# Recurrent mixer's end: outputs of two chunks at a time, q's squares added on VectorE, two gate tiles behind the sums

## The reference, cut to what matters

```python
def step(state, xs):                       # one chunk n, all heads
    qg_n, kdec_n, w_n, u_n, attn_n, gl_n = xs
    v_new = u_n - einsum('bhcd,bhde->bhce', w_n, state)
    o = einsum('bhcd,bhde->bhce', qg_n, state) + einsum('bhij,bhje->bhie', attn_n, v_new)
    state = state * gl_n[..., None, None] + einsum('bhcd,bhce->bhde', kdec_n, v_new)
    return state, o
...
q = q * rsqrt(sum(q * q, -1, keepdims=True) + NORM_EPS)       # before the rule
...
o = o * rsqrt(mean(o * o, -1, keepdims=True) + NORM_EPS) * norm_g
o = o * silu(z)
return o.reshape(b, s, C_WIDTH) @ w_out
```

## Time and profile before

| what | value |
|---|---|
| time, median of 3 runs | 2130.39 us (2130.28 to 2131.53) |
| span of the profiled execution | 2131.0 us; no other time of it is given |
| mean granted TensorE clock | 0.996 |
| TensorE, weight loads, VectorE, ScalarE busy | 2102.4, 1905.9, 1492.2, 1111.1 us |
| chain that ended last, by engine | TensorE 89%, VectorE 5%, ScalarE 4%, issue 1% |
| data moved | 359.28 MB, 169 GB/s on average |

### The profile page before, as it was taken

How to read it: one execution, slowest core, us unless ns; L and a number is a source line. 1 busy time by engine, 2 the same in 40 slices (tenths; PEclk the granted TensorE clock), 3 DMA queues, 4 the chain that set the end, 5 groups by cost and what they waited for, 6 DMA issues and landing times.

```text
span 2131.0 us, 36321 instructions
## 1 busy us (share of the span) xinstructions
PE 2102.4 (99%) x15424; PEld 1905.9 (89%) x15424; DVE 1492.2 (70%) x2246; ACT 1111.1 (52%) x1749; POOL 8.6 (0%) x14
## 2 busy tenths in 40 slices
PE   9999999999999999999999999999999999999998
PEld 8999899999999999899998887988888899888997
DVE  5777867777677676467777558665555678778776
ACT  5445664446444654464447658353333467666454
POOL 0000000000000000000000000000000000000000
PEclk9999999999999999999999999999999999999999
DMA  8665445664566422156653211234443444214541
GB/s 330 244 255 208 164 180 220 239 256 169 225 255 241 171 102 87 60 209 231 254 226 119 99 61 41 78 141 158 157 155 149 175 174 152 106 41 178 195 182 60
DMA packets 51282, 359.28 MB, mean 169 GB/s; under 512 B 5680, under 2 KB 5808, under 8 KB 8496
## 3 DMA queue, kind: packets, MB, share of 16 engines
q1 hardware_dynamic: 49680, 351.30, 43.8%
q10 hardware_dynamic: 1440, 5.65, 0.7%
HBM read 355.88 MB, written 1.05 MB: 167 GB/s over the span
## 4 chain that ended last, share of the span: by engine, by line
PE 89%; DVE 5%; ACT 4%; issue 1%; DMA 0%; SPq 0%; ACTq 0%; DVEq 0%
PE ps L1030 9%; PE ps L1029 9%; PE ps L1028 9%; PE ps L3007 5%; PE ps L3009 5%; PE ps L3008 5%; PE ps L1112 4%; PE ps L1113 4%; PE ps L1114 4%; PE ps L461 2%; PE ps L462 2%; PE ps L463 2%; PE ps L1329 2%; PE ps L1344 2%; PE ps L2670 2%; PE ps L2672 2%
## 5 line engine op out<-in xcount | busy, mean ns | idle before, releaser
L400 DVE TENSOR_TENSOR wl<-ring,wh 128x1024 fp32r<-128x1024 f32 x380 | 452.8, 1220 | 161.8 <-ACT wh L394 161.6
L1028 PE MATMUL ps<-xs,wh 128*128 128x256 f32 x1664 | 471.1, 283 | 1.2 <-DVE wl L434 0.9
L1030 PE MATMUL ps<-xs,wh 128*128 128x256 f32 x1664 | 470.9, 283 | 0.0
L1029 PE MATMUL ps<-xs,wl 128*128 128x256 f32 x1664 | 470.9, 283 | 0.0
L394 ACT ACTIVATE wh<-ring 128x1024 fp32r<-128x1024 f32 x380 | 379.5, 1050 | 96.4 <-PE ps L1114 72.8
L1028 PEld LDWEIGHTS ps<-xs,wh 128*128 128x128 f32 x1664 | 319.0, 192 | 5.9 <-DVE wl L434 1.8
L1029 PEld LDWEIGHTS ps<-xs,wl 128*128 128x128 f32 x1664 | 319.0, 192 | 4.1 <-issue 0.2
L1030 PEld LDWEIGHTS ps<-xs,wh 128*128 128x128 f32 x1664 | 319.0, 192 | 0.0
L1112 PE MATMUL ps<-wh,hh 128*128 128x512 f32 x440 | 173.0, 393 | 0.8 <-DVE hl L1227 0.8
L1113 PE MATMUL ps<-wl,hh 128*128 128x512 f32 x440 | 172.4, 392 | 0.0
L1114 PE MATMUL ps<-wh,hl 128*128 128x512 f32 x440 | 171.2, 389 | 0.0
(11 more groups left out here) (577 smaller groups left out, 4488.0 us busy)
## 6 DMA issues: line engine op xcount, KB each, us to landing
ring<-wstream SPq DMA_DIRECT2D x331, 1024.0 KB, 4.9
cond_ctx<-crow ACTq DMA_DIRECT2D x3, 512.0 KB, 10.3
CN<-consts ACTq DMA_DIRECT2D x1, 1056.0 KB, 9.1
X<-xin SPq DMA_DIRECT2D x4, 256.0 KB, 5.6
ring<-wstream SPq DMA_DIRECT2D x4, 256.0 KB, 6.5
ring<-wstream SPq DMA_DIRECT2D x2, 512.0 KB, 8.8
X<-cin ACTq DMA_DIRECT2D x1, 1024.0 KB, 8.6
out<-X SPq DMA_DIRECT2D x4, 256.0 KB, 2.9
```

The source lines that it names most:

```text
L400: dve.tensor_tensor(lo, w, hi.bitcast(F32), ALU.subtract).then_inc(low_part, tiles_done)
L1028: pe.matmul(out, wh[:, w, c, :], x_hi, start=start, stop=False, skip_group_check=True)
L1029: pe.matmul(out, wl[:, w, c, :], x_hi, start=False, stop=False, skip_group_check=True)
L1030: return pe.matmul(out, wh[:, w, c, :], x_lo, start=False, stop=True, skip_group_check=True)
```

## The change

TensorE's outputs are taken apart: `outputs_of_state(c, b)` holds the eight matmuls with the state, and `outputs_of_pair(g, banks)` does the products with V of the two chunks of pair g together, alternating head by head between rows 0 to 63 and rows 64 to 127, each chunk into its own bank. The order becomes: state 1, pair 0, tile 29, from_state 3, states 2 and 3, pair 1, means 0 to 3, tile 30, tile 31, output projection. q's squares are no longer multiplied with the ones on TensorE: VectorE adds them to o's (`sum_of_squares`), and a mean is one matmul. On ScalarE the squares, the table load, the last two gate tiles and the high part of tile 34 change places, on VectorE the low part of tile 34. Some banks change.

```diff
@@ -202,7 +202,7 @@
 LN_HALF = {"l0_1c": 1, "l0_2c": 1}
 LN_BANKS = {"l0_1c": (0, 1), "l0_2x": (0, 1), "ab": (6, 7), "c": (6, 7), "l1_1": (6, 7)}
 LN_LATE = LNS[2:]
-C_BANK = [BANK_ORDER[t % 4] for t in range(12)] + [1 - t % 2 for t in range(12, 31)] + [5]
+C_BANK = [BANK_ORDER[t % 4] for t in range(12)] + [1 - t % 2 for t in range(12, 30)] + [5, 7]
 POOLED = ["ab"]
 PAIR0 = {name: sum(2 if k in POOLED else 4 for k in LNS[0:i]) for i, name in enumerate(LNS)}
 MOMENTS = LNS[0:2] + LNS[6:7]
@@ -1889,16 +1889,17 @@
         c_s1 = sem("c_first_state")
         c_att_p, c_att_v = sem("c_attention_tensor"), sem("c_attention_vector")
         c_qg, c_qsq = sem("c_q_decayed"), sem("c_q_squared")
-        c_o_p = Steps(sem("c_out_tensor"), ["o0", "o1", "o2", "var0", "o3", "var1", "var2", "var3"])
+        c_o_p = Steps(sem("c_out_tensor"), [f"o{c}" for c in range(4)] + [f"var{c}" for c in range(4)])
         c_o_a = Steps(sem("c_out_scalar"), [f"sq{c}" for c in range(4)] + [x for c in range(4) for x in (f"ln{c}", f"rn{c}")])
-        c_o_v = Steps(sem("c_out_vector"), [f"r{c}" for c in range(4)] + [f"z{n}" for n in range(4)])
+        c_o_v = Steps(sem("c_out_vector"), [f"sum{c}" for c in range(4)] + [f"r{c}" for c in range(4)]
+                      + [f"z{n}" for n in range(4)])
 
         def pe_mixer_c():
             t0 = TILE0["c_k"]
 
             def tile(t):
-                if t == 31:
-                    pe.wait_ge(*c_o_a.at("ln0"))
+                if t >= 30:
+                    pe.wait_ge(*c_o_a.at(f"ln{t - 30}"))
                 elif t >= 26:
                     pe.wait_ge(c_z_a, t - 25)
                 elif t >= 4:
@@ -1982,25 +1983,25 @@
                                        stop=True, skip_group_check=True)
                     mm.then_inc(*c_scan_p(("WS", c, q)))
 
-            def outputs(c, b):
-                r, g = RS[c % 2], c // 2
+            def outputs_of_state(c, b):
+                pe.wait_ge(c_qg, 4)
+                for h in range(8):
+                    pe.matmul(ps[:, b, h * CH:(h + 1) * CH], S[c][:, h, :], c_eg[:, h, cs(c)], start=(h == 0), stop=False,
+                              skip_group_check=True)
+
+            def outputs_of_pair(g, banks):
+
                 pe.wait_ge(c_att_v, g + 1)
-                if c:
-                    pe.wait_ge(c_qg, 4)
-                    pe.wait_ge(*c_scan_v.at(("v", c, 1)))
-                    for h in range(8):
-                        pe.matmul(ps[:, b, h * CH:(h + 1) * CH], S[c][:, h, :], c_eg[:, h, cs(c)], start=(h == 0),
-                                  stop=False, skip_group_check=True)
                 for h in range(8):
-                    mm = pe.matmul(ps[:, b, h * CH:(h + 1) * CH], V[r, h, g, :], attnT[r, g, h, :], start=(c == 0),
-                                   stop=True, skip_group_check=True)
-                mm.then_inc(*c_o_p(f"o{c}"))
+                    for n, r in enumerate(RS):
+                        mm = pe.matmul(ps[:, banks[n], h * CH:(h + 1) * CH], V[r, h, g, :], attnT[r, g, h, :],
+                                       start=(g == 0 and n == 0), stop=True, skip_group_check=True)
+                        if h == 7:
+                            mm.then_inc(*c_o_p(f"o{2 * g + n}"))
 
             def mean_of_squares(c, b):
-                pe.wait_ge(c_qsq, 4)
-                pe.wait_ge(*c_o_a.at(f"sq{c}"))
-                pe.matmul(ps[:, b, :], ones, c_q[:, :, cs(c)], start=True, stop=False)
-                pe.matmul(ps[:, b, :], ones, o_sq[:, c, :, :], start=False, stop=True).then_inc(*c_o_p(f"var{c}"))
+                pe.wait_ge(*c_o_v.at(f"sum{c}"))
+                pe.matmul(ps[:, b, :], ones, o_sq[:, c, :, :], start=True, stop=True).then_inc(*c_o_p(f"var{c}"))
 
             pe_three_tiles(t0, BANK_ORDER[0:3], x_parts("c"), normed="ffn1_1")
             pe_wait_ple(1, "a")
@@ -2116,21 +2117,23 @@
             state_product(2)
             pe.wait_ge(c_att_v, 1)
             chunk_products(2, 1, c_q).then_inc(c_att_p, 1)
-            outputs(0, 4)
+            pe.wait_ge(*c_scan_v.at(("v", 1, 1)))
+            outputs_of_state(1, 6)
+            outputs_of_pair(0, (4, 6))
             tile(29)
             from_state(3)
-            outputs(1, 6)
+            pe.wait_ge(c_att_v, 2)
+            outputs_of_state(2, 2)
+            outputs_of_state(3, 3)
+            pe.wait_ge(*c_scan_v.at(("v", 3, 1)))
+            outputs_of_pair(1, (2, 3))
+            mean_of_squares(0, 5)
+            mean_of_squares(1, 7)
+            pe.wait_ge(c_z_a, 5)
+            mean_of_squares(2, 1)
+            pe.wait_ge(c_z_a, 6)
+            mean_of_squares(3, 0)
             tile(30)
-            pe.wait_ge(c_att_v, 2)
-            outputs(2, 2)
-            pe.wait_ge(*c_scan_v.at(("v", 3, 1)))
-            mean_of_squares(0, 5)
-            outputs(3, 7)
-            mean_of_squares(1, 3)
-            pe.wait_ge(c_z_a, 6)
-            mean_of_squares(2, 1)
-            pe.wait_ge(c_z_a, 7)
-            mean_of_squares(3, 0)
             tile(31)
             pe.wait_ge(*c_o_a.at("ln3"))
             pe_three_tiles(TILE0["c_out"], (0, 1, 2), x_parts("c2"), xo, third=lambda: pe.wait_ge(c_z_a, 8))
@@ -2314,17 +2317,15 @@
             for k in range(4):
                 act.activation(flat(c_q, k), flat(c_q, k), ACT.Square, scale=(P * 1e-6) ** 0.5).then_inc(c_qsq, 1)
             square_o(0, 4)
+            square_o(1, 6)
             act_high(t0 + 32)
             z_tile(5)
-            square_o(1, 6)
             act_high(t0 + 33)
-            z_tile(6)
-            act_high(t0 + 34)
             act.preload_act_table_set("natural_log_exp_and_others")
             square_o(2, 2)
-            square_o(3, 7)
+            square_o(3, 3)
             norm_o(0, 5)
-            norm_o(1, 3)
+            norm_o(1, 7)
             norm_o(2, 1)
             norm_o(3, 0)
             act.preload_act_table_set("silu_and_others")
@@ -2333,9 +2334,11 @@
                 act.wait_ge(*c_o_v.at(f"z{k}"))
                 act.activation(xo[:, 2 * k:2 * k + 2, 0, :], c_o[:, 2 * k:2 * k + 2, :], ACT.Copy).then_inc(x_high, 1)
 
-            z_tile(7)
+            z_tile(6)
+            act_high(t0 + 34)
             o_high(0)
             o_high(1)
+            z_tile(7)
             o_high(2)
             o_high(3)
             act_high(t0 + 35)
@@ -2414,6 +2417,11 @@
             def decayed_q(k):
                 dve.wait_ge(c_silu, 24)
                 dve.tensor_tensor(flat(c_eg, k), flat(c_eg, k), flat(c_q, k), ALU.mult).then_inc(c_qg, 1)
+
+            def sum_of_squares(c):
+                dve.wait_ge(c_qsq, 4)
+                dve.wait_ge(*c_o_a.at(f"sq{c}"))
+                dve.tensor_tensor(o_sq[:, c, :, :], o_sq[:, c, :, :], c_q[:, :, cs(c)], ALU.add).then_inc(*c_o_v(f"sum{c}"))
 
             def scaled_o(c, b):
                 dve.wait_ge(*c_o_a.at(f"rn{c}"))
@@ -2569,17 +2577,21 @@
             attention(1)
             new_values(3)
             dve_low(t0 + 32)
+            sum_of_squares(0)
+            sum_of_squares(1)
             dve_low(t0 + 33)
-            dve_low(t0 + 34)
+            sum_of_squares(2)
+            sum_of_squares(3)
             scaled_o(0, 4)
             scaled_o(1, 6)
             scaled_o(2, 2)
-            scaled_o(3, 7)
+            scaled_o(3, 3)
             dve.wait_ge(*c_o_v.at("r3"))
             dve.wait_ge(c_z_a, 6)
             gated_o(0)
             gated_o(1)
             gated_o(2)
+            dve_low(t0 + 34)
             dve.wait_ge(c_z_a, 8)
             gated_o(3)
             o_low(0)
```

## The result

The changed kernel takes 2120.12 us in the median of 4 runs (2119.58 to 2120.60) against 2130.93 (2130.28 to 2131.53): ratio 0.9948, interval 0.9936 to 0.9960, so 10.8 us faster. I had said 2122.7 and a range from 2120.6.

The account below looks back on a forecast made before the run. TensorE, busy 99% of the span, was taken as the bound. Pairs -3.8, q's squares -3.5, shorter stand -0.4 and fewer edges -0.0 to 0.2 made -7.7: 2130.39 to 2122.7 us, range 2120.6 to 2125.2.

Parts of the forecast that it names:

- Pairing, 3.8 us: Outputs on TensorE: two alternating pairs take 3.88 us instead of 7.68, at 0.06 us an instruction; 3.8 us removed.
- q's squares, 3.5 us: Means of squares: four fp32 matmuls leave TensorE for VectorE additions, about 3.5 us removed.
- Two gate tiles as cover: Tiles 30 and 31 behind the means: 5.76 us of TensorE work, to 892.01, while ScalarE's tail runs.
- The tail on ScalarE: Logarithms and exponentials at 1.42 us a pair, table load, gate tile: projection starts at 892.85, 7.7 us earlier.
- The stand: TensorE's wait just ahead of the output projection: about 0.7 us instead of 1.08, counted as 0.4 us gained.
- TensorE's own list: TensorE's work in program order from 868.11; alone it would let the projection start at 892.0, a gain of 8.5.
- my sum: The new order added up step by step from 868.11 to the projection's start at 892.85; 7.7 us gained.
- The projection behind it: In the 29.48 us behind the changed stretch TensorE has no gap, so the shift should arrive whole.
- The clock: The stretch from first output to projection, 32.41 us, was read at granted clock 1.00 (2.4 GHz).
- Rival 3: Behind the change, a 1.7 us clock fall may come or go (2121.0 or 2124.4), or half the shift arrives (2126.5); 7%.

Follow-up runs that it names:

- the filled kernel: Kernel before in its own order, each half-row output product alternating with an unused product on the other half of the rows; 2130.58 us, ratio 0.9996.
- before_again: The kernel before, run again unchanged; 2131.61 us, ratio 0.9999.
- after_again: The changed kernel, run again unchanged; 2121.34 us, ratio 0.9953 against the kernel before.

## Why the prediction was right or wrong, step by step

- **Pairing, 3.8 us.** Right: 1.93 us a pair against 1.94 said. Adding onto the state's part alternates as freely as opening a sum.
- **q's squares, 3.5 us.** Right: four means in 3.54 us (0.96 + 3 x 0.86); put back on TensorE they cost 3.2. The sums on VectorE delayed nothing.
- **Two gate tiles as cover.** Right, and needed: with one tile 1.9 us come back, and the squares alone lose 1.3 of 3.5.
- **The tail on ScalarE.** Mis-sized. I took 1.42 us a pair from 891.75 to 893.17; but 893.17 is 0.2 us behind the end of mean 1 at 892.97, so that row held a wait for TensorE. Without it a pair takes 1.25 us (and 890.83 was 0.07 above its own terms, 888.85 + 0.63 + 1.28), so gate tile 6 starts 7.54 us behind pair 1 (879.43 to 886.97) and not 8.12 (882.71 to 890.83): 0.6 us. The stand is 0.26 us by the step, where I had 0.84 (892.01 to 892.85). With TensorE's own list 0.16 us shorter than my sum, the stretch is 24.00 us, not 24.74, and lost 8.4 us, not 7.7. In the terms of my sum: by the step the stand before was 1.24 us (899.16 + 0.12 to 900.52), so 1.0 went where I had 0.4.
- **The projection behind it.** Right: 29.48 us without a gap in both kernels.
- **The clock.** This is the step that failed: "at granted clock 1.00", read from one execution and taken for the median, so that the sum had the clock inside the stretch at nothing. The mis-sized tail alone, 0.7 us, would have made the forecast 2122.0, against 2120.1. Rival 3 looked for falls behind the change, either way; they were inside the stretch of the kernel before, in four traces of seven, at 3.17 us each time, so about 1.8 us on average; by the filled kernel, which loses little else, it is about 1.2. In none of the four traces of the changed kernel are they there.
- **The rest.** Of the 11.4 us between the means of the table (10.8 between the medians of the first comparison) 8.4 are the stretch at full clock, 1.2 to 1.8 the falls in it (both are estimates), and 0.35 a stand of VectorE at another place (below). Some 0.8 to 1.4 us is left. Falls outside the stretch, most of them near 256, 720 to 750 and 1920 to 1933 us, come and go with the execution in both kernels: 18 in the seven traces of the kernel before, 7 in the four of the changed one, so 2.6 a trace against 1.8. At some 1.6 us a fall (half of 3.17) that would be enough, but four traces do not tell whether the changed kernel has fewer. That stays open.

## What to carry over

Before a row is taken as the price of an operation, look whether its start is a handoff: a step that begins 0.2 us behind another engine's end holds that engine's time. Two products that each use half of the rows of the array cost half when they alternate, also where they add onto earlier sums, and the cover that hid the old tail has to be moved with them. One trace tells one execution's clock: where a kernel's runs spread by 5 us, take several traces before the stretch is priced.

## What the runs showed of the hardware that I had not expected

- The granted clock fell from 2.4 to 1.2 GHz in stretches where the profile shows TensorE busy without a gap (4.00 of 4.00 us, and 6.80 of 6.80). The Trainium skill, TensorE: Matmul & The Clock Gate, section Part 1: The HAM clock gate, says that the clock is set by how busy TensorE has been recently; the busy share of the profile's rows does not show that measure, since these falls came at a full share, behind work on half of the rows.
- Half rows are not the only such work. In all seven traces of the kernel before the clock also falls near 724 us, behind 3.6 us of matmuls of 16 columns on all 128 rows, again without a gap (0.79 and 8.00 of 8.00 us busy from 720 to 728 in the first). TensorE's timeline there, kernel before; the next tile goes at 0.21 us a matmul:

```profile
719.99 3.78 PE L2013 MATMUL ps<-ring,X 128*128 128x16 f32 x32
723.61 0.56 PE L461 MATMUL ps<-xs,wh 128*128 128x256 f32 x1
723.97 0.41 PE L462 MATMUL ps<-xs,wl 128*128 128x256 f32 x1
724.18 0.41 PE L463 MATMUL ps<-xs,wh 128*128 128x256 f32 x1
```

- Sixteen more matmul instructions an output, on the other half of the rows, cost 0.01 us each time (32.44 against 32.41 for four of them).
- The kernels fall into two groups that differ by 0.35 us at one place far behind the change, the same in all traces of a kernel. VectorE stands 0.47 us ahead of one instruction in the kernel before and not in the changed one; nothing there was edited, and the cause was not looked for. Before (before_again), then changed (after_again):

```profile
1398.48 0.69 DVE L759 TENSOR_TENSOR xc<-xc_whole,xc 128x512 fp32r<-128x512 f32 x1 [0.47 <-DVE xc_whole L754]
```

```profile
1387.76 0.69 DVE L759 TENSOR_TENSOR xc<-xc_whole,xc 128x512 fp32r<-128x512 f32 x1
```
